# The last mixer's convolution norm: its sums move to GpSimd, its root to columns, its gate behind the head loop

## The chip, the core and the metric

The kernel runs on one core of one Trainium2 chip. The metric is the device time of one execution in microseconds. A core has TensorE (matmuls; its weight loads have a row of their own), VectorE, ScalarE, GpSimd and a queue of transfers; in the traces they are PE (PEld), DVE, ACT, POOL and SP. They run side by side and wait for each other by semaphores.

## What is computed

Two blocks of two layers each over 512 tokens of width 1024, all in float32. The change concerns the odd mixer of the second block, the last one in the program. Its reference, cut to what matters:

```python
def odd_mixer(h, w_in, dw_w, dw_b, ln_g, ln_b, conv_w, conv_b, A_log, dt_bias, D_skip, norm_w, w_out):
...
    g = glu_a * jax.nn.sigmoid(glu_b)
    g = depthwise_conv(g, dw_w, dw_b, CONV_K // 2, CONV_K // 2)
    g = jax.nn.silu(layer_norm(g, ln_g, ln_b))
    xbc = jax.nn.silu(depthwise_conv(xbc, conv_w, conv_b, SSM_CONV // 2, SSM_CONV - 1 - SSM_CONV // 2))
...
    y_f = ssd_scan(xs, dt[:, :, 0], A[0], Bm, Cm)
    y_b = flip(ssd_scan(flip(xs), flip(dt[:, :, 1]), A[1], flip(Bm), flip(Cm)))
    y = (y_f + y_b + xs * D_skip.astype(jnp.float32)[:, None]).reshape(b, S, SSM_INNER)
    y = rms_norm(y * jax.nn.silu(z.astype(jnp.float32)), norm_w).astype(h.dtype)
    return jnp.concatenate([g, y], axis=-1) @ w_out
```

The filter of `g` has 31 taps (CONV_K) on 512 channels, that of `xbc` four on 2048; the scan has 16 heads in four groups.

`layer_norm` subtracts the mean over the 512 channels and multiplies by the reciprocal root of the mean square plus 1e-6.

## The kernel before

Channels lie on the 128 partitions and tokens along the free dimension, so a tile is 128 x 512 and the 512 channels of `g` are four tiles `CO[0]` to `CO[3]`. All projections stream their weights in chunks of 128 output channels: a transfer fills `w_raw`, ScalarE writes the high part (`split_high`, L323), GpSimd the low part (`pool_stream`, L335), and TensorE does three products for each of eight input tiles (`product`, L374). High and low parts have two buffers, so a chunk's high part can be written once the chunk two before it has been multiplied. The order is written out by hand, engine by engine, in `odd_pe`, `odd_act`, `odd_dve` and `pool_stream`; every engine works its list strictly in order.

In the mixer come the chunks of g and its gate, one of dt, 16 of xbc and 8 of z, and then the output product in two parts: `o_out_g` (8 chunks of half depth, from g) and `o_out_y` (8 chunks, from y). Meanwhile the long filter's 31 taps are computed: VectorE (`taps`, L2768) does tiles 0 and 1 and 20 taps of tile 2, with the running sum in PSUM banks 5 and 6; ScalarE writes the products of tile 3 and of the 11 other taps of tile 2 (`tap_terms`, L2368) and GpSimd adds them up (`pool_taps`, L2378). In each chunk's step ScalarE has the high part of the weights first and the products second, GpSimd the low part first and the adds second. `conv_sum` (L2790) and `activated` are the short filter of xbc.

Behind the chunks comes the prologue of the scan: scores of head group 0 (L2469), decay rows of heads 0 and 1 (L2496, L2498), the four column sums of g (L2519), the products carried between token blocks (`carried`, L2482 and L2484), the mean (L2833), the four subtractions (L2836), four squares on ScalarE (L2650) with their sums on TensorE (L2524), mean square (L2840) and root (L2652). Then 16 head steps: ScalarE writes a head's weights (`decays`, L2638), VectorE adds the two directions (L2848) and multiplies by the scores (L2850), TensorE multiplies by x (`pair`, L2530), VectorE finishes a pair of heads (`finish`, L2824 and L2827). In between lie, for each group of four heads, `scaled_rows` (L2807) and `from_carried` (L2817). Reciprocal and scaling of the norm stand in steps 0 and 1 (L2853, L2857), Silu and high parts of g behind ScalarE's step 7 (L2660, L2663), low parts in VectorE's step 10 (L2862). GpSimd only squares the finished y (`pool_squares`, L2385 and L2388). Behind the loop come the sum for y's norm (L2549, L2551), the first part of the output product, the reciprocal (L2877), and y in high and low parts (L2881, L2891).

`YOFF` lies in `rope_sb` and `square_sum`, `CO` and the filter's input in `y_space`, `TERM`, `L_SUM` and the decay weights in `arena`, `XS`, `CBS` and `OM` in `x_space`. G is the PSUM: banks 4 and 5 serve scores and carried products in turn (`ring`).

## Time and profile before

| | us |
|---|---|
| median of 3 runs | 3685.42 |
| lowest, highest run | 3682.53, 3688.09 |
| profiled execution, its own time | 3684.6 |
| its span, first to last instruction | 3682.8 |
| TensorE busy in the span | 3565.9 (97%) |
| VectorE busy | 1784.2 (48%) |
| ScalarE busy | 1278.2 (35%) |
| GpSimd busy | 1492.9 (41%) |
| stretch 3112 to 3135 (prologue of the scan), TensorE busy | 19.53 of 23.00 |
| stretch 3135 to 3208 (head steps), TensorE busy | 59.06 of 73.00 |
| the same, VectorE and ScalarE busy | 61.52 and 46.95 |

Positions in the text are microseconds from the start of the span. The page of the profile gives busy times by engine; the chain of waits follows the work that ended last back to what released it; the timeline lists an engine's instructions in order, with the idle time before one in brackets and the engine that ended it. The span is 1.8 us shorter than the execution's own time.

### The profile page before, as it was taken

How to read it: one execution, taken by the hardware profiler on the slowest of the kernel's cores; microseconds unless marked ns; L12 is line 12 of the kernel's file. 1: busy time of each engine (PE TensorE's matmuls, PEld its weight loads, DVE VectorE, ACT ScalarE, POOL GpSimd, SP SyncE). 2: the span in 40 equal slices, each digit the busy share in tenths (PEclk: the TensorE clock that was granted, in tenths of full speed). 3: DMA queues.
4: the chain of work that ended last, by engine and by line, in shares of the span. 5: the costliest groups of instructions: out<-in, count | busy, mean ns of one | idle time of the engine just before them, and what ended most of it. 6: DMA issues, size and time to landing. Idle time of an engine off the chain costs nothing.

```text
span 3682.8 us, 54791 instructions
## 1 busy us (share of the span) xinstructions
PE 3565.9 (97%) x20592; PEld 3064.8 (83%) x20592; DVE 1784.2 (48%) x2350; ACT 1278.2 (35%) x2142; POOL 1492.9 (41%) x661
## 2 busy tenths in 40 slices
PE   8999999999988999999999999999999999899998
PEld 8988999999966888888887888888888876588886
DVE  3773664447555444632246442335233587753234
ACT  3643332222264222422233532224222455542222
POOL 3331444443402444444452234444444465244443
PEclk9999999999998999999999999999999999999999
DMA  4220222222201222222232112232222222022222
GB/s 147 78 75 30 87 87 92 88 90 87 86 24 46 94 96 95 88 92 91 97 109 75 47 57 97 91 100 89 97 91 97 92 86 69 7 98 94 95 95 82
DMA packets 86428, 307.38 MB, mean 83 GB/s; under 512 B 9568, under 2 KB 11872, under 8 KB 86112
## 3 DMA queue, kind: packets, MB, share of 16 engines
q1 hardware_dynamic: 85824, 303.69, 24.6%
q8 instruction: 135, 2.21, 0.3%
q10 hardware_dynamic: 416, 1.05, 0.1%
q14 instruction: 53, 0.43, 0.0%
HBM read 302.60 MB, written 2.10 MB: 83 GB/s over the span
## 4 chain that ended last, share of the span: by engine, by line
PE 86%; DVE 8%; ACT 3%; DVEq 1%; issue 1%; POOL 0%; DMA 0%; ACTq 0%; SPq 0%; POOLq 0%
PE psum L374 71%; PE psum L586 6%; PE psum L604 1%; DVE arena L1170 1%; PE psum L624 1%; PE psum L2097 1%; DVE arena L1201 1%; PE psum L1308 1%; DVE psum L2790 0%; PE psum L1326 0%; DVE scale L666 0%; PE psum L2061 0%; DVE square_sum L491 0%; PE psum L2081 0%; ACT arena L2638 0%
## 5 line engine op out<-in xcount | busy, mean ns | idle before, releaser
L335 POOL TENSOR_TENSOR w_lo<-w_raw,w_hi 128x1024 fp32r<-128x1024 f32 (+1 forms) x507 | 1262.0, 2490 | 1787.8 <-ACT w_hi L323 1787.7
L323 ACT ACTIVATE w_hi<-w_raw 128x1024 fp32r<-128x1024 f32 (+1 forms) x507 | 533.8, 1053 | 1842.6 <-PE psum L374 1831.4
L374 PE MATMUL psum<-x_hi,w_hi 128*128 128x512 f32 (+1 forms) x2744 | 902.0, 357 | 12.7 <-POOL w_lo L335 8.4
L374 PE MATMUL psum<-x_lo,w_hi 128*128 128x512 f32 (+1 forms) x2744 | 902.6, 357 | 0.0
L374 PE MATMUL psum<-x_hi,w_lo 128*128 128x512 f32 (+1 forms) x2744 | 898.4, 356 | 0.0
L374 PE MATMUL psum<-y_hi,w_hi 128*128 128x264 f32 (+1 forms) x2272 | 634.9, 329 | 11.8 <-DVE arena L1179 3.4
L374 PE MATMUL psum<-y_lo,w_hi 128*128 128x264 f32 (+1 forms) x2272 | 634.3, 329 | 0.0
L374 PE MATMUL psum<-y_hi,w_lo 128*128 128x264 f32 (+1 forms) x2272 | 631.8, 328 | 0.0
L374 PEld LDWEIGHTS psum<-x_hi,w_hi 128*128 128x128 f32 x2744 | 485.4, 188 | 96.3 <-POOL w_lo L335 9.7
L374 PEld LDWEIGHTS psum<-x_lo,w_hi 128*128 128x128 f32 x2744 | 484.5, 188 | 78.7 <-issue 1.4
L374 PEld LDWEIGHTS psum<-x_hi,w_lo 128*128 128x128 f32 x2744 | 485.1, 189 | 76.5
L374 PEld LDWEIGHTS psum<-y_hi,w_hi 128*128 128x128 f32 x2272 | 383.8, 189 | 55.6 <-issue 6.8
L374 PEld LDWEIGHTS psum<-y_lo,w_hi 128*128 128x128 f32 x2272 | 383.0, 189 | 38.9 <-issue 0.5
L374 PEld LDWEIGHTS psum<-y_hi,w_lo 128*128 128x128 f32 x2272 | 383.1, 189 | 38.0
L1045 DVE TENSOR_TENSOR arena<-psum,arena 128x512 f32<-128x512 f32 x88 | 60.9, 692 | 393.8 <-PE psum L374 387.5
L1049 DVE TENSOR_TENSOR y_lo<-arena,y_hi 128x512 f32 x88 | 193.5, 2199 | 90.5 <-ACT y_hi L1017 90.5
L420 DVE TENSOR_TENSOR arena<-psum,scale 128x512 f32<-128x512 f32 (+1 forms) x80 | 55.7, 697 | 296.0 <-PE psum L374 296.0
L335 POOL TENSOR_TENSOR w_resident<-w_raw,w_resident 128x1024 fp32r<-128x1024 f32 (+1 forms) x50 | 108.5, 2191 | 190.8 <-DVE x_lo L874 108.0
L406 DVE TENSOR_TENSOR arena<-psum,scale 128x512 f32 (+3 forms) x68 | 47.0, 697 | 271.5 <-PE psum L374 270.0
L966 DVE TENSOR_TENSOR y_lo<-arena,y_hi 128x528 f32 (+1 forms) x64 | 152.8, 2388 | 18.2 <-ACT y_hi L935 16.8
L1043 DVE TENSOR_TENSOR arena<-psum,scale 128x512 f32<-128x512 f32 x88 | 60.8, 691 | 135.9 <-PE psum L374 134.9
L961 DVE TENSOR_SCALAR arena<-psum 128x528 f32<-128x528 f32 (+1 forms) x64 | 44.8, 699 | 107.9 <-PE psum L374 98.3
(510 smaller groups left out, 4280.8 us busy)
## 6 DMA issues: line engine op xcount, KB each, us to landing
w_raw<-in_weights SPq DMA_DIRECT2D x566, 512.0 KB, 3.3
resid<-in_xT SPq DMA_DIRECT2D x8, 264.0 KB, 8.0
out_dram<-resid SPq DMA_DIRECT2D x16, 128.0 KB, 1.7
arena<-in_lru_w SPq DMA_DIRECT2D x1, 1024.0 KB, 10.1
rope_sb<-in_rope SPq DMA_DIRECT2D x1, 528.0 KB, 11.4
rope_sb<-in_rope ACTq DMA_DIRECT2D x1, 512.0 KB, 4.7
y_space<-in_pool_inv ACTq DMA_DIRECT2D x1, 512.0 KB, 6.1
mats<-in_mats SPq DMA_DIRECT2D x1, 448.0 KB, 10.5
```

Of the source, the lines that this page charges most:

```text
L323: nc.scalar.activation(weight_parts(n, i, c)[0][:, 0:w], RAW[:, (n + c) % 4, 0:w], ACT.Copy).then_inc(high_ready, 1)
L335: nc.gpsimd.tensor_tensor(wl[:, 0:w], RAW[:, (n + c) % 4, 0:w], wh[:, 0:w], ALU.subtract).then_inc(low_ready, 1)
L374: last = mm(o[:, a, :], wt[:, k * P:k * P + P], x[:, k, a * (w // banks):(a + 1) * (w // banks)], start=(k == 0 and p == 0), stop=(k == kt ...
L406: take(dve, n, count, lambda ps, i, c: tt(toks(dst[:, 4 * i + c, offset:offset + w], n), ps, toks(RS[:, 0:w], n), ALU.mult))
L420: tt(toks(t, n), acc(n, c), toks(RS[:, 0:w], n), ALU.mult).then_inc(psum_free, 1)
L586: last = mm(G[:, (n + c) % 4, half(h)], w[:, k * P:k * P + P], x[:, k, half(h)], start=(k == 0 and q == 0), stop=(k == kt - 1 and q == 2))
L604: mm(G[:, 4, half(h)], ones[:, :], PREP_SQ[m % 4], start=(k == 0), stop=(k == DT - 1)).then_inc(wide_summed, 1)
L961: ts(toks(SCR[:, 2 + c % 2, 0:w], n), ps, 0.0, None, ALU.max).then_inc(psum_free, 1)
L966: tt(YL[:, 4 * i + c, 0:w], SCR[:, c % 2, 0:w], YH[:, 4 * i + c, 0:w], ALU.subtract).then_inc(h_low, 1)
L1043: tt(SCR[:, 2 + c // 2, 0:T2], acc(n, c)[:, 0, :], RS[:, 0:T2], ALU.mult).then_inc(psum_free, 1)
L1045: tt(SCR[:, c // 2, 0:T2], acc(n, c)[:, 0, :], SCR[:, 2 + c // 2, 0:T2], ALU.mult).then_inc(psum_free, 1)
L1049: tt(YL[:, 2 * j + c // 2, 0:T2], SCR[:, c // 2, 0:T2], YH[:, 2 * j + c // 2, 0:T2], ALU.subtract).then_inc(h_low, 1)
```

## The change

- The long filter: VectorE does 16 taps of tile 2 in place of 20 and keeps the running sum in `CO[2]` (SBUF) in place of PSUM. GpSimd adds up the other 15 in a scratch tile `PART2`; they start one chunk earlier than its taps did and end two chunks later. VectorE adds `PART2` at the end.
- In all chunk steps of xbc and z ScalarE has its tap products ahead of the high part of the weights, and GpSimd its adds ahead of the low part.
- The sums: GpSimd adds the four tiles of g (`pool_moments`), one matmul sums over the channels, VectorE writes the mean; GpSimd subtracts it from the four tiles, squares and adds the squares, in eleven operations.
- The root: four one-column matmuls put the sums of squares in four columns (tokens on the partitions); VectorE adds the small constant and makes a first guess from the bits; GpSimd refines it by three Newton steps of four operations on 128 x 4 elements, ahead of its second square of y; four matmuls spread the roots over a bank, ScalarE copies it to SBUF ahead of its step 10. No square root and no reciprocal of full tiles is left in this norm.
- The scaling of the four tiles goes to VectorE's steps 10 to 13; Silu, high parts and low parts of g go behind the loop. The first chunk of `o_out_g` stands ahead of the last matmul of y's norm and waits for g's parts tile by tile.
- The order of the two PSUM banks of the ring is shifted once for group 2 and back for group 3, and the scores wait for the bank's new users.

```diff
@@ pool_stream
                     for n in range(a, b):
+                        pool_taps(pool, n - CHUNKS["xbc"] - 3)
+                        if n == CHUNKS["o_out_g"] + 1:
+                            pool_moments(pool)
                         if n == CHUNKS["o_out_g"] + 2:
                             pool_squares(pool)
                         one(n, 0, 0)
-                        pool_taps(pool, n - CHUNKS["xbc"] - 3)
...
+        PART2, L_SUM, L_SQ, L_RSTD = (SCR[:, i, 0:T2] for i in (5, 4, 5, 4))
+        L_VAR, L_ROOT, L_STEP = (COL[:, 96 + 4 * i:100 + 4 * i] for i in range(3))
+
+        def pool_sum(f):
+            return PART2 if f == 2 else CO[f]
+
+        def ring(use):
+
+            return 4 + (use + (use >= 14) + (use >= 21)) % 2
+
+        POOL_TAPS = [(3, j) for j in range(CONV_K)] + [(2, j) for j in range(16, CONV_K)]
...
-                nc.gpsimd.tensor_tensor(CO[f], CO[f], TERM[k % 2], ALU.add).then_inc(st["o_pt"], 1)
+                nc.gpsimd.tensor_tensor(pool_sum(f), pool_sum(f), TERM[k % 2], ALU.add).then_inc(st["o_pt"], 1)
+
+        def pool_moments(pool):
+
+            pool.wait_ge(st["o_gc"], 2)
+            pool.drain()
+            nc.gpsimd.tensor_tensor(L_SUM, CO[0], CO[1], ALU.add)
+            pool.drain()
+            nc.gpsimd.tensor_tensor(L_SUM, L_SUM, CO[3], ALU.add)
+            pool.drain()
+            pool.wait_ge(st["o_gc"], 3)
+            nc.gpsimd.tensor_tensor(L_SUM, L_SUM, CO[2], ALU.add).then_inc(st["o_ln"], 1)
+            pool.wait_ge(st["o_xm"], 1)
+            for f in range(4):
+                nc.gpsimd.tensor_tensor(CO[f], CO[f], MU, ALU.subtract)
+                pool.drain()
+                last = nc.gpsimd.tensor_tensor(GSQ if f else L_SQ, CO[f], CO[f], ALU.mult)
+                pool.drain()
+                if f:
+                    last = nc.gpsimd.tensor_tensor(L_SQ, L_SQ, GSQ, ALU.add)
+                    pool.drain()
+            last.then_inc(st["o_ln"], 1)
 
         def pool_squares(pool):
 
             for f in range(DT - 1):
+                if f == 1:
+                    pool.wait_ge(st["o_xm"], 2)
+                    for _ in range(3):
+                        nc.gpsimd.tensor_tensor(L_STEP, L_ROOT, L_ROOT, ALU.mult)
+                        pool.drain()
+                        nc.gpsimd.tensor_tensor(L_STEP, L_STEP, L_VAR, ALU.mult)
+                        pool.drain()
+                        nc.gpsimd.tensor_scalar(L_STEP, L_STEP, -0.5, 1.5, ALU.mult, ALU.add)
+                        pool.drain()
+                        last = nc.gpsimd.tensor_tensor(L_ROOT, L_ROOT, L_STEP, ALU.mult)
+                        pool.drain()
+                    last.then_inc(st["o_ln"], 1)
...
-        TAP_ORDER = [(f, j) for j in range(1, CONV_K) for f in (0, 1)] + [(2, j) for j in range(20)]
+        TAP_ORDER = [(f, j) for j in range(1, CONV_K) for f in (0, 1)] + [(2, j) for j in range(16)]
...
         def tap_sum(f):
-            return G[:, 6 if f else 5, :]
+            return CO[2] if f == 2 else G[:, 5 + f, :]
@@ odd_pe
-            pe.wait_ge(st["o_gc"], 1)
-            for f in range(4):
-                last = mm(G[:, 6, :], ones[:, :], CO[f], start=(f == 0), stop=(f == 3))
-            last.then_inc(st["o_mu"], 1)
+            pe.wait_ge(st["o_ln"], 1)
+            mm(G[:, 6, :], ones[:, :], L_SUM, start=True, stop=True).then_inc(st["o_st"], 1)
             carried(0)
-            for f in range(4):
-                pe.wait_ge(sq_in, f + 1)
-                mm(G[:, 7, :], ones[:, :], GSQ, start=(f == 0), stop=(f == 3)).then_inc(sum_in, 1)
+
+            def squared_columns():
+
+                pe.wait_ge(st["o_ln"], 2)
+                pe.wait_ge(st["o_oe"], 5)
+                for j in range(NB):
+                    last = mm(G[:, 4, j:j + 1], L_SQ[:, P * j:P * j + P], ones[:, 0:1], start=True, stop=True)
+                last.then_inc(st["o_st"], 1)
+
+            def roots_spread():
+
+                pe.wait_ge(st["o_ln"], 3)
+                pe.wait_ge(st["o_oe"], 8)
+                for j in range(NB):
+                    last = mm(G[:, 4, P * j:P * j + P], L_ROOT[:, j:j + 1].broadcast_to([P, P]), ident[:, :], start=True,
+                              stop=True)
+                last.then_inc(st["o_st"], 1)
...
+                if f == 2:
+                    squared_columns()
+                if f == 4:
+                    roots_spread()
...
             mm(G[:, 4, :], ones[:, :], Y_SUM, start=True, stop=False)
-            pe.wait_ge(sq_in, 4 + 1)
+            n = CHUNKS["o_out_g"]
+            product(pe, n, 1, YH, YL, kt=4, parts=SPLIT_AT["o_g"][0])
+            pe.wait_ge(sq_in, 1)
@@ odd_act
             for c in range(16):
+                tap_terms(act, c - 1)
                 split_high(act, CHUNKS["xbc"] + 2, 0, c)
-                tap_terms(act, c - 1)
...
             decays(0)
             decays(1)
-            act.wait_ge(st["o_xm"], 1)
-            for f in range(4):
-                if f:
-                    act.wait_ge(sum_in, f)
-                nc.scalar.activation(GSQ, CO[f], ACT.Square).then_inc(sq_in, 1)
-            act.wait_ge(var_in, 1)
-            nc.scalar.activation(SCR[:, 5, 0:T2], SCR[:, 4, 0:T2], ACT.Sqrt).then_inc(std_in, 1)
+            split_high(act, CHUNKS["z"] + 2, 0, DT - 1)
             for h in range(2, SSM_HEADS):
+                if h == 10:
+                    act.wait_ge(st["o_st"], 3)
+                    nc.scalar.activation(L_RSTD, G[:, 4, :], ACT.Copy).then_inc(st["o_lc"], 1)
                 decays(h)
                 if h % HG == 2 and h // HG + 1 < SSM_GROUPS:
                     score_copies(h // HG + 1)
-                if h == 7:
-                    act.wait_ge(st["o_g"], 1)
-                    for f in range(4):
-                        nc.scalar.activation(CO[f], CO[f], ACT.Silu, bias=vec("ln_b", f))
-                    act.drain()
-                    for f in range(4):
-                        nc.scalar.activation(YH[:, f, 0:T2], CO[f], ACT.Copy).then_inc(h_high, 1)
+            for f in range(4):
+                act.wait_ge(st["o_g"], f + 1)
+                nc.scalar.activation(CO[f], CO[f], ACT.Silu, bias=vec("ln_b", f))
+                act.drain()
+                nc.scalar.activation(YH[:, f, 0:T2], CO[f], ACT.Copy).then_inc(h_high, 1)
@@ odd_dve
                     dve.wait_ge(st["o_pt"], adds(len(POOL_TAPS)))
-                    tt(CO[2], CO[2], tap_sum(2), ALU.add)
+                    tt(CO[2], CO[2], PART2, ALU.add).then_inc(st["o_gc"], 1)
...
-            dve.wait_ge(st["o_mu"], 1)
-            ts(MU, G[:, 6, :], 1.0 / 512, None, ALU.mult)
-            dve.drain()
-            for f in range(4):
-                last = tt(CO[f], CO[f], MU, ALU.subtract)
-            last.then_inc(st["o_xm"], 1)
+            dve.wait_ge(st["o_st"], 1)
+            ts(MU, G[:, 6, :], 1.0 / 512, None, ALU.mult).then_inc(st["o_xm"], 1)
             from_carried(0)
-            dve.wait_ge(sum_in, 4)
-            ts(SCR[:, 4, 0:T2], G[:, 7, :], 1.0 / 512, EPS, ALU.mult, ALU.add).then_inc(var_in, 1)
             for h in range(SSM_HEADS):
                 g, w, m = h // HG, W[h % 2], OM[h % 2]
+                if h == 4:
+                    dve.wait_ge(st["o_st"], 2)
+                    ts(L_VAR, G[:, 4, 0:NB], 1.0 / 512, EPS, ALU.mult, ALU.add)
+                    dve.drain()
+                    ts(L_ROOT.bitcast(I32), L_VAR.bitcast(I32), -0.5, 1597463007.0, ALU.mult,
+                       ALU.add).then_inc(st["o_xm"], 1)
...
-                if h == 0:
-                    dve.wait_ge(std_in, 1)
-                    nc.vector.reciprocal(SCR[:, 4, 0:T2], SCR[:, 5, 0:T2])
-                if h == 1:
-                    dve.drain()
-                    for f in range(4):
-                        last = stt(CO[f], CO[f], vec("ln_g", f), SCR[:, 4, 0:T2], ALU.mult, ALU.mult)
-                    last.then_inc(st["o_g"], 1)
-                if h == 10:
-                    for f in range(4):
-                        dve.wait_ge(h_high, SPLIT_AT["o_g"][0] + f + 1)
-                        tt(YL[:, f, 0:T2], CO[f], YH[:, f, 0:T2], ALU.subtract).then_inc(h_low, 1)
+                if 10 <= h < 14:
+                    f = h - 10
+                    if f == 0:
+                        dve.wait_ge(st["o_lc"], 1)
+                    stt(CO[f], CO[f], vec("ln_g", f), L_RSTD, ALU.mult, ALU.mult).then_inc(st["o_g"], 1)
...
+            for f in range(4):
+                dve.wait_ge(h_high, SPLIT_AT["o_g"][0] + f + 1)
+                tt(YL[:, f, 0:T2], CO[f], YH[:, f, 0:T2], ALU.subtract).then_inc(h_low, 1)
             finish(DT - 1)
```

ScalarE in the step of xbc chunk 5 before; `y_space` to `arena` are the tap products, `arena` from `arena` is a logarithm for dt:

```order
L2571 ACTIVATE arena<-psum 128x512 [waits o_cv]
L323 ACTIVATE w_hi<-w_raw 128x1024 [waits tile_done,raw_loaded1]
L2368 ACTIVATE arena<-y_space,vecs_sb 128x512 [waits o_pt] x2
L2587 ACT_TABLE_LOAD
L2587 ACTIVATE arena<-arena 128x128 [waits o_dt]
L2594 ACTIVATE psum<-arena,vecs_sb 128x512 [waits o_xe,o_si]
```

and in the change:

```order
L2637 ACTIVATE arena<-psum 128x512 [waits o_cv]
L2379 ACTIVATE arena<-y_space,vecs_sb 128x512 [waits o_pt] x2
L323 ACTIVATE w_hi<-w_raw 128x1024 [waits tile_done,raw_loaded1]
L2653 ACT_TABLE_LOAD
L2653 ACTIVATE arena<-arena 128x128 [waits o_dt]
L2660 ACTIVATE psum<-arena,vecs_sb 128x512 [waits o_xe,o_si]
```

The high part of the weights has moved behind the two products.

GpSimd at the end of the z chunks before; `w_lo` are low parts of the weights, `y_space` from `y_space` and `arena` the adds of taps, `x_space` from `arena` the squares of y:

```order
L335 TENSOR_TENSOR w_lo<-w_raw,w_hi 128x1024
L2378 TENSOR_TENSOR y_space<-y_space,arena 128x512 x2
L335 TENSOR_TENSOR w_lo<-w_raw,w_hi 128x1024 x2
L2385 TENSOR_TENSOR x_space<-arena 128x512 x2
L2388 TENSOR_TENSOR x_space<-x_space 128x512
```

and in the change, up to the first square of g:

```order
L335 TENSOR_TENSOR w_lo<-w_raw,w_hi 128x1024
L2389 TENSOR_TENSOR arena<-arena 128x512 x2
L2395 TENSOR_TENSOR arena<-y_space 128x512
L2397 TENSOR_TENSOR arena<-arena,y_space 128x512
L2400 TENSOR_TENSOR arena<-arena,y_space 128x512
L2403 TENSOR_TENSOR y_space<-y_space,scale 128x512
L2405 TENSOR_TENSOR arena<-y_space 128x512
L2403 TENSOR_TENSOR y_space<-y_space,scale 128x512
```

The adds go on for two chunks longer, and the sums of g stand between them and the last low part.

VectorE from the last add of the filter to step 1 before; `x_space` from `arena` 128x1024 are scaled rows, the pairs of `x_space` 128x512 the head steps, `rope_sb` and `square_sum` the reads of carried products:

```order
L2774 TENSOR_TENSOR y_space<-y_space,psum 128x512
L2807 TENSOR_TENSOR x_space<-arena 128x1024 x3
L2833 TENSOR_SCALAR scale<-psum 128x512
L2836 TENSOR_TENSOR y_space<-y_space,scale 128x512 x4
L2817 TENSOR_TENSOR rope_sb<-psum,arena 128x512 x2
L2817 TENSOR_TENSOR square_sum<-psum,arena 128x512
L2840 TENSOR_SCALAR arena<-psum 128x512
L2848 TENSOR_TENSOR x_space<-arena 128x512
L2850 TENSOR_TENSOR x_space<-x_space 128x512
L2853 RECIPROCAL arena<-arena 128x512
L2848 TENSOR_TENSOR x_space<-arena 128x512
L2850 TENSOR_TENSOR x_space<-x_space 128x512
```

and in the change:

```order
L2835 TENSOR_TENSOR y_space<-y_space,arena 128x512
L2867 TENSOR_TENSOR x_space<-arena 128x1024 x3
L2892 TENSOR_SCALAR scale<-psum 128x512
L2876 TENSOR_TENSOR rope_sb<-psum,arena 128x512 x2
L2876 TENSOR_TENSOR square_sum<-psum,arena 128x512
L2907 TENSOR_TENSOR x_space<-arena 128x512
L2909 TENSOR_TENSOR x_space<-x_space 128x512
L2907 TENSOR_TENSOR x_space<-arena 128x512
L2909 TENSOR_TENSOR x_space<-x_space 128x512
L2867 TENSOR_TENSOR x_space<-arena 128x1024 x3
```

The subtractions, the mean square, the reciprocal and the scaling are gone from here.

## Rows read from the trace of the kernel before

**Rows 1.** Chain of waits: start us, us, engine, buffer, line, count.
```profile
3116.68 3.45 PE psum L2519 x8
...
3243.41 18.48 PE psum L374 x78
```

**Rows 2.** Stretches: window, its us, busy us and count per engine, PEclk, DMA share, GB/s.
```profile
3072.00:3076.00 4.00, 3.72 (x12) 3.15 (x13) 3.76 (x6) 3.30 (x6) 2.69 (x2) 0.57 0.03 6
3112.00:3135.00 23.00, 19.53 (x64) 10.11 (x64) 14.39 (x20) 13.33 (x33) 1.67 (x1) 1.00 0.06 23
3135.00:3208.00 73.00, 59.06 (x369) 40.28 (x367) 61.52 (x73) 46.95 (x148) 19.16 (x13) 0.98 0.00 1
```

**Rows 3.** Timeline, GpSimd and VectorE: start us, us, engine, line, operation, count.
```profile
3220.29 2.96 POOL L335 TENSOR_TENSOR w_lo<-w_raw,w_hi 128x512 fp32r<-128x512 f32 x2 [3.98 <-ACT w_hi L323]
...
3222.20 1.60 DVE L2881 SCALAR_TENSOR_TENSOR arena<-arena,vecs_sb 128x512 f32<-128x512 f32 x1
...
3238.79 2.99 DVE L2881 SCALAR_TENSOR_TENSOR arena<-arena,vecs_sb 128x512 f32<-128x512 f32 x1
...
3238.83 2.40 POOL L335 TENSOR_TENSOR w_lo<-w_raw,w_hi 128x1024 fp32r<-128x1024 f32 x1 [0.68 <-ACT w_hi L323]
```

**Rows 4.** One line's instructions: duration ns minimum, median, maximum; first, last start.
```profile
L2768 DVE SCALAR_TENSOR_TENSOR psum<-y_space,vecs_sb,psum x77: 748/755/759, 2962.1 to 3114.2; 128x512 f32<-128x512 f32 x77
```

**Rows 5.** Timeline of ScalarE, GpSimd, TensorE, VectorE around xbc chunks 7 and 10.
```profile
2995.91 1.06 ACT L323 ACTIVATE w_hi<-w_raw 128x1024 fp32r<-128x1024 f32 x1 [0.17 <-issue]
...
2996.87 1.32 ACT L2368 ACTIVATE arena<-y_space,vecs_sb 128x512 f32<-128x512 f32 x2
...
2997.04 2.35 POOL L335 TENSOR_TENSOR w_lo<-w_raw,w_hi 128x1024 fp32r<-128x1024 f32 x1 [7.60 <-ACT w_hi L323]
...
2999.45 0.79 PE L374 MATMUL psum<-x_hi,w_hi 128*128 128x512 f32 x1 [6.60 <-POOL w_lo L335]
...
3025.63 0.69 DVE L2782 TENSOR_TENSOR arena<-psum,scale 128x512 f32<-128x512 f32 x1 [0.19 <-PE psum L374]
```

**Rows 6.** Timeline, end of the z chunks: GpSimd add, VectorE taps, last eviction.
```profile
3103.34 1.28 POOL L2378 TENSOR_TENSOR y_space<-y_space,arena 128x512 f32<-128x512 f32 x1 [0.16 <-issue]
...
3104.91 4.91 DVE L2768 SCALAR_TENSOR_TENSOR psum<-y_space,vecs_sb,psum 128x512 f32<-128x512 f32 x6
...
3110.12 0.69 DVE L2796 TENSOR_TENSOR y_space<-psum,scale 128x512 f32<-128x512 f32 x1 [0.31 <-PE psum L374]
```

**Rows 7.** Timeline of TensorE: behind an idle time; first and last carried products of group 0.
```profile
3072.28 1.09 PE L2446 MATMUL psum<-ident,arena 128*128 128x128 f32 x4 [5.21 <-ACT arena L2602]
...
3119.95 0.59 PE L2482 MATMUL psum<-x_space 128*128 128x256 f32 x2
...
3125.53 0.59 PE L2484 MATMUL psum<-x_space 128*128 128x256 f32 x2
```

**Rows 8.** Timeline of VectorE: head steps 0, 1, 4 and 15.
```profile
3133.17 0.68 DVE L2848 TENSOR_TENSOR x_space<-arena 128x512 f32<-128x512 f32 x1
...
3134.53 3.35 DVE L2853 RECIPROCAL arena<-arena 128x512 f32<-128x512 f32 x1
...
3139.28 2.74 DVE L2857 SCALAR_TENSOR_TENSOR y_space<-y_space,vecs_sb,arena 128x512 f32<-128x512 f32 x4
...
3154.13 0.69 DVE L2848 TENSOR_TENSOR x_space<-arena 128x512 f32<-128x512 f32 x1 [0.40 <-PE psum L2530]
...
3203.39 1.37 DVE L2850 TENSOR_TENSOR x_space<-x_space 128x512 f32<-128x512 f32 x1
```

**Rows 9.** Timeline of VectorE (step 8, step 10, behind the loop); line L521 on TensorE.
```profile
3173.06 0.69 DVE L2848 TENSOR_TENSOR x_space<-arena 128x512 f32<-128x512 f32 x1 [1.05 <-ACT arena L2638]
...
3183.78 2.49 DVE L2862 TENSOR_TENSOR y_lo<-y_space,y_hi 128x512 fp32r<-128x512 f32 x4
...
3214.85 3.34 DVE L2877 RECIPROCAL arena<-arena 128x512 f32<-128x512 f32 x1
...
L521 PE MATMUL psum<-ones,square_sum x38: 238/250/261, 23.2 to 1193.3; 128*128 128x1 f32 x38
```

56 lines of the change are left out of this document (28 added, 28 removed).

## The prediction

> **What bounds the kernel now.** I began with the busy shares: TensorE 97%, so over the span the matmuls are the bound and only a stretch where TensorE waits can move the end. The chain of waits shows where that is near the change: while the last mixer's convolutions are formed, it runs through VectorE; in the scan's prologue it goes through the four column sums of the norm (the first of [rows 1]), then through the squares, which ScalarE and TensorE do in turn; from there it goes through the 16 head steps and a norm to 3243.41, where the output product at last runs without a wait (the second of [rows 1]). In the stretches of the table TensorE is 85% busy in the prologue (19.53 of 23.00 us) and 81% in the head steps, while VectorE has 61.52 of 73.00 us [rows 2]. So the head steps go by VectorE and the hand-overs round it, not by matmuls. GpSimd has 19.16 us there, and the change gives it more. That makes the meeting of VectorE and GpSimd the question.
>
> **What they do to each other.** Two halves of a split (1.29 us each) took 2.96 us together when a VectorE instruction came between them; that VectorE instruction and the one behind it were held until GpSimd ended: 1.60 us where 0.75 is usual, and 2.99 us against a split of 2.40 us [rows 3]. Both read two tensors from SBUF. The convolution's multiply-add with its running sum in PSUM never shows it: 77 of them lie between 748 and 759 ns though GpSimd's adds (1.28 us, the next one 0.16 us behind [rows 6]) and splits run all through that stretch [rows 4]. So an instruction with both inputs in SBUF takes turns with GpSimd. Price of a turn: with a 1.29 us operation the pair takes 2.96 - 1.29 = 1.67 us where VectorE alone needs 4.91/6 = 0.82 [rows 6], so +0.85; with a 2.40 us split, by the same 1.67 - 1.29 = 0.38, 2.40 + 0.38 - 0.82 = +1.96.
>
> The Trainium skill (SBUF — State Buffer, Who interferes with whom) states the same lock for two SBUF inputs and speaks against this change in one more point: it counts only the inputs, so moving a tap's running sum out of PSUM is enough to bring the lock in. By that rule the term for the taps below is 8.7 us; without it that term is nothing.
>
> **Part 1, order of weights and taps.** Every step now issues ScalarE's tap products ahead of its high part of the weights, and GpSimd's two adds ahead of the low part. Mostly the products run while ScalarE would wait for TensorE anyway. At 2995.91 they can't: ScalarE is late, its high part is at once followed by GpSimd's low part, and TensorE, idle for 6.60 us, starts at 2999.45 [rows 5]. Now the first product is ready at 2995.91 + 0.7 = 2996.6, two adds take 2 x (1.29 + 0.16) = 2.9 us [rows 6], the low part 2.35: TensorE starts at 3001.9, +2.5 us. The next chunks have slack against VectorE, but at 3025.63 VectorE waits 0.19 us for TensorE [rows 5], and behind it the chain is VectorE's. Term: **+2.5**. Bounds: 0 (if the start hides) and 2.9.
>
> **Part 2, taps.** VectorE's taps of tile 2 go from 20 to 16 (-4 x 0.82 = -3.3 us at the end), but all now have both inputs in SBUF: 3 in the step of z chunk 4, 6 in each of chunks 5 and 6, one tap and the final add in the last. Against the 15 ahead of the eviction of chunk 7 stand six adds, one sum and two splits: 7 x 0.85 + 2 x 1.96 = 9.8 us, less 1.1 us of idle time ahead of three evictions (0.31 ahead of the last [rows 6]): 8.7. The eviction of chunk 7 goes from 3110.12 [rows 6] to 3118.8. ScalarE's Silu of that chunk, the score copies and the decay rows hang on it.
>
> **Part 3, prologue.** Removed from its path: three of the four sums (3.45 us for four, 0.86 each [rows 1]), the four subtractions, four squares and four sums of squares, the mean of squares. TensorE reached the sums 3116.68 - 3110.12 = 6.6 us behind the eviction; now 3118.8 + 6.6 = 3125.4, plus 0.86 for the one sum, plus the carried products, 3119.95 to 3126.12 = 6.2 us [rows 7], plus 0.7 for VectorE's last read: the first head step at 3133.2, where it was 3133.17 [rows 8]. So everything gained is spent on the taps. TensorE is now idle for some 6 us before the scores; behind the 5.21 us of idle time that ended at 3072.28 the granted clock was 0.57 for 4 us, near the lower of its two levels, 1.2 GHz [rows 2, 7]. That costs 0 to 1.7 us; I take **+0.8**. The sum on GpSimd waits for the last tap; it is done before TensorE asks.
>
> **Part 4, head steps 0 to 3.** They took 3154.13 - 3133.17 = 20.96 us [rows 8]. Out: the reciprocal 3.35 and the scaling 2.74 (-6.1). In: GpSimd's eleven operations on means and squares begin when the mean is written, 6.3 us before the first head step; at 1.45 us each four are over, seven are left. The seven VectorE instructions of steps 0 and 1 and of the scaled rows, all with two SBUF inputs, pay 7 x 0.85 = 6.0; then one split (+1.96) and the first square (+0.6): 8.6. At step 4 VectorE waits for four one-column matmuls (0.25 us each [rows 9]) and does two small instructions: +1.5. GpSimd's wait for this blocks the squares of y behind it, which have the rest of the loop. Term: -6.1 + 8.6 + 1.5 = **+4.0**. Bounds: -4.6 (no turn taken) and +6.5 (each turn priced as 2.99 - 0.75 = 2.24 for splits and 1.3 for the rest).
>
> **Part 5, the rest of the loop.** ScalarE's Silu and casts leave the loop: the 1.05 us that VectorE waited at 3173.06 go [rows 9], -1.05. Twelve small GpSimd operations: +0.7 by turns. At step 10 four low parts (2.49) go, two scalings of 0.75 come: -1.0. Two more in steps 12 and 13, one in idle time: +0.8. The spread of roots falls into ScalarE's former delay: 0. Sum **-0.55**.
>
> **Part 6, behind the loop.** Four Silu and four casts now follow the last decay, beside VectorE's last products, but the four low parts (2.49 us [rows 9]) stand ahead of the last finish and partly wait for ScalarE: I take 2.2 us. Against that the reciprocal no longer waits for a chunk of the output product: it started 3214.85 - 3204.76 = 10.1 us behind the last head step (3203.39 + 1.37 [rows 8]); now 3.1 for the finish as before, 2.2 for the push, 3.4 for square, sum, mean and root of 0.6 to 1.0 each: 8.7. Term: **-1.4**; bounds -3 and +2.
>
> **Sum.** 2.5 + 0.8 + 4.0 - 0.55 - 1.4 = +5.35 us. The profiled execution is 3684.6 us (span 3682.8); 3684.6 + 5.4 = 3690. The median of the runs, 3685.4, is 0.8 us above it; I leave that to the range. The clock, here 0.98 to 1.00 in the loop and prologue [rows 2], is taken as unchanged but for the 0.8.
>
> **Rivals.**
> (A) *The taps take no turn*, because VectorE gets in between GpSimd's operations: the eviction stays at 3110.12, TensorE has no long idle time ahead of the scores, the loop still pays. Time: 3690 - 8.7 - 0.8 = 3680.5. Against it: every two-input row beside a GpSimd one is held.
> (B) *Neither pays*: also part 4's 8.6 goes: 3672. Only if the held rows had another cause; no row speaks for it.
> (C) *The roots come too late*, slower. GpSimd is asked for a reciprocal square root in twelve operations, between step 4 and the spread ahead of step 10's decays, about 19 us (3154.13 to 3173). It has no row for so small an operation nor for a scalar one. Between 0.16 and 1.45 us each (the gap alone, a whole 128x512 add) the twelve need 2 to 17 us; it decides from 19 us on: then TensorE stands in front of the decays and each microsecond counts in full. With the first scalar operation costing as much as several adds, 8 us late: 3698. The Trainium skill (GPSIMD Engine Reference, Instruction dispatch) names about 6 us for the first call of freshly loaded code, and the order shows a load ahead of this first scalar operation; by that price alone, 6 + 12 x 0.5, it would still fit, and the sum stays.
> (D) *The wait of part 1 is hidden*: 3687.5, within the forecast's own range.
>
> **How the numbers follow.** The forecast with D (3684 to 3696): 60%. A: 16%, B: 7%, C: 17%. A measurement of this kernel can tell 0.2%, 7.4 us, from no change: below 3678.0 is faster, above 3692.8 slower. Faster: B and 5 of A: 12%. Same: 42 of the forecast, 11 of A, 2 of C: 55%. Slower: 18 of the forecast, 15 of C: 33%. Range 3677 to 3699: leaves out B and the end of A below, the far half of C above.
>
> **What would show it.** Taps of tile 2 in SBUF at 1.3 to 2.9 us in place of 0.75, and chunk 7's eviction 8 to 9 us later against the chunks' product; TensorE's start at 2999 moved by 2.5; the two-input instructions of steps 0 and 1 at 1.3 to 1.7 us; 25 us from step 0 to 4; the reciprocal 8.7 us behind the last step. The forecast is wrong if the taps keep 0.75 us, if the first head step comes before 3130, or if TensorE stands in front of step 10's decays.

## The result, and the profile after

| | before | after |
|---|---|---|
| median of 12 runs, us | 3685.19 | 3692.25 |
| lowest, highest run | 3682.53, 3688.09 | 3687.95, 3696.70 |
| ratio, 95% interval | | 1.0016 (1.0008 to 1.0023) |
| profiled execution: span, mean granted clock | 3682.8, 0.992 | 3691.1, 0.988 |
| head steps, from step 0 to the end of step 15 | 71.59 | 77.26 |

After is 7.06 us slower: less than the 0.2% that this kernel's measurement can tell apart, though the interval excludes equal times. 3690 was forecast. That the sum came out is worth little by itself, since two of its terms were wrong by 2 us and more in opposite directions. So the traces are compared term by term.

The program ahead of the stage is the same in both, yet the stage begins at different positions, so all positions are counted from VectorE's first read of xbc chunk 0. These two rows of the timeline (start us, us, engine, line, operation, output and inputs, shape, count) are that point, of before and of after:

```profile
2961.33 0.69 DVE L2782 TENSOR_TENSOR arena<-psum,scale 128x512 f32<-128x512 f32 x1
...
2962.50 0.69 DVE L2843 TENSOR_TENSOR arena<-psum,scale 128x512 f32<-128x512 f32 x1
```

| us | before | after | difference | forecast | after, second profile |
|---|---|---|---|---|---|
| first read to eviction of z chunk 2 | 118.77 | 118.66 | -0.1 | +2.5 (part 1) | 119.10 |
| z chunk 2 to z chunk 7 | 30.02 | 38.06 | +8.0 | +8.7 (part 2) | 38.07 |
| z chunk 7 to head step 0 | 23.05 | 14.15 | -8.9 | -8.7 +0.8 (part 3) | 14.44 |
| head step 0 to 4 | 20.96 | 24.92 | +4.0 | +4.0 (part 4) | 24.92 |
| head step 4 to the end of 15 | 50.63 | 52.34 | +1.7 | -0.55 (part 5) | 52.34 |
| to the reciprocal | 10.09 | 10.17 | +0.1 | -1.4 (part 6) | 8.71 |
| to the uninterrupted output product | 28.56 | 29.87 | +1.3 | 0 | 28.60 |
| to the end of the span | 439.39 | 440.43 | +1.0 | 0 | 438.92 |
| sum | 721.47 | 728.60 | +7.1 | +5.35 | 725.10 |

The last column is a profile of the same kernel after, taken with the experiments below. By it the stage is 3.6 us longer than in before, not 7.1: its head steps agree, what follows them does not. Before has one profile, so a difference of 1 us in a row of this table rests on one execution on each side.

**Part 1.** TensorE's timeline in after, at the late low part and at the next long idle time (the brackets give the idle time before a row and what ended it), and VectorE's eviction of z chunk 2 in before and in after:

```profile
3002.88 0.79 PE L376 MATMUL psum<-x_hi,w_hi 128*128 128x512 f32 x1 [6.58 <-POOL w_lo L335]
...
3074.93 0.63 PE L2490 MATMUL psum<-ident,arena 128*128 128x128 f32 x4 [2.59 <-ACT arena L2668]
...
3080.10 0.69 DVE L2796 TENSOR_TENSOR y_space<-psum,scale 128x512 f32<-128x512 f32 x1 [3.85 <-PE psum L374]
...
3081.16 0.69 DVE L2857 TENSOR_TENSOR y_space<-psum,scale 128x512 f32<-128x512 f32 x1 [2.25 <-PE psum L376]
```

TensorE starts 40.38 us behind the first read where it was 38.12, so the wait forecast as 2.5 is there with 2.3 [rows 5]. But TensorE's wait behind the last xbc chunk, which ends with a tile from ScalarE (L2668), fell from 5.21 [rows 7] to 2.59 us. It ends 112.43 us behind the first read, 1.5 us later than in before (110.95), so part of the delay is still there. The work from there to the eviction took 7.82 us in before, where the granted clock was 0.57 from 3072 to 3076 [rows 2], and takes 6.23 us in after at 1.00: 1.6 us come back by the clock, and VectorE's wait at z chunk 2 is as much shorter (3.85 and 2.25 us). The second profile of after has the restart 0.4 us late and 7.79 us of work behind it, the six experiments that leave both orders as in after have 1.1 to 1.4 and 6.2 us. What became of the rest of the 2.3 us stands at p1_old_order below.

**Part 2.** VectorE's taps of tile 2 beside z chunks 5 and 6, and the evictions of chunks 6 and 7; before had 4.91 us for six taps and the last eviction at 3110.12 [rows 6]:

```profile
3101.16 10.04 DVE L2829 SCALAR_TENSOR_TENSOR y_space<-y_space,vecs_sb 128x512 f32<-128x512 f32 x6
3111.12 0.68 DVE L2857 TENSOR_TENSOR y_space<-psum,scale 128x512 f32<-128x512 f32 x1
3111.89 7.41 DVE L2829 SCALAR_TENSOR_TENSOR y_space<-y_space,vecs_sb 128x512 f32<-128x512 f32 x6
3119.22 0.68 DVE L2857 TENSOR_TENSOR y_space<-psum,scale 128x512 f32<-128x512 f32 x1
```

A tap takes 10.04 / 6 = 1.67 us on average, beside two adds and parts of two splits (L335 at 3100.37 and 3106.37); single ones of the 15 taps in SBUF take 0.75 to 2.75 us.

**Part 3.** TensorE at the scores and at the one column sum, and VectorE's first head step:

```profile
3121.27 3.67 PE L2516 MATMUL psum<-arena 128*128 128x512 f32 x4 [4.99 <-ACT x_space L2694]
...
3126.53 1.02 PE L2565 MATMUL psum<-arena,ones 128*128 128x512 f32 x2
...
3133.37 0.68 DVE L2907 TENSOR_TENSOR x_space<-arena 128x512 f32<-128x512 f32 x1
```

The one sum stands where four stood [rows 1]. Step 0 starts 0.2 us behind its old position in the span [rows 8], and 1.0 us ahead of it when both are counted from the first read. The four scores take 3.67 us where they took 1.98 in before (L2469 at 3112.95), behind 4.99 us of idle time: TensorE ran near 1.2 GHz there (granted clock 0.64 from 3112 to 3121, 0.79 from 3121 to 3130). The sum so comes 7.31 us behind the eviction of z chunk 7 where 6.56 was worked out, 0.75 us late. The carried products take 5.3 us (3127.39 to 3132.72) where they took 6.2 with a wait of 0.60 us for VectorE among them.

**Part 4.** Steps 2 and 4 on VectorE, and GpSimd's last add of squares and the split beside step 2:

```profile
3145.16 1.75 DVE L2907 TENSOR_TENSOR x_space<-arena 128x512 f32<-128x512 f32 x1
3146.99 2.69 DVE L2909 TENSOR_TENSOR x_space<-x_space 128x512 f32<-128x512 f32 x1
...
3157.92 0.16 DVE L2898 TENSOR_SCALAR columns<-psum 128x4 f32<-128x4 f32 x1 [1.31 <-PE psum L2573]
...
3144.30 2.06 POOL L2408 TENSOR_TENSOR arena<-arena,x_space 128x512 f32<-128x512 f32 x1
3146.52 2.61 POOL L335 TENSOR_TENSOR w_lo<-w_raw,w_hi 128x1024 fp32r<-128x1024 f32 x1 [0.16 <-issue]
```

Each of VectorE's two instructions stands until the one of GpSimd is over: 3146.99 + 2.69 and 3146.52 + 2.61 end 0.55 us apart. Step 4's columns wait 1.31 us for TensorE.

**Part 5.** GpSimd's squares of y behind the Newton steps with the two VectorE instructions beside them, and the same meeting at the gate of step 11:

```profile
3166.88 1.04 POOL L2429 TENSOR_TENSOR x_space<-arena 128x512 f32<-128x512 f32 x1 [0.16 <-issue]
3168.07 1.53 POOL L2432 TENSOR_TENSOR x_space<-x_space 128x512 f32<-128x512 f32 x1
...
3167.18 1.29 DVE L2907 TENSOR_TENSOR x_space<-arena 128x512 f32<-128x512 f32 x1 [1.21 <-issue]
3168.54 1.60 DVE L2909 TENSOR_TENSOR x_space<-x_space 128x512 f32<-128x512 f32 x1
...
3192.02 1.53 POOL L2432 TENSOR_TENSOR x_space<-x_space 128x512 f32<-128x512 f32 x1
3192.34 1.75 DVE L2914 SCALAR_TENSOR_TENSOR y_space<-y_space,vecs_sb,arena 128x512 f32<-128x512 f32 x1
```

**Part 6.** VectorE's four low parts and the last finish, the reciprocal, and TensorE's mean and the start of the uninterrupted product:

```profile
3210.55 3.56 DVE L2924 TENSOR_TENSOR y_lo<-y_space,y_hi 128x512 fp32r<-128x512 f32 x4
3214.04 0.73 DVE L2883 SCALAR_TENSOR_TENSOR arena<-arena,vecs_sb,psum 128x512 f32<-128x512 f32 x1
...
3220.80 3.35 DVE L2932 RECIPROCAL arena<-arena 128x512 f32<-128x512 f32 x1
...
3218.36 1.02 PE L2617 MATMUL psum<-arena,ones 128*128 128x512 f32 x2
...
3250.67 0.54 PE L376 MATMUL psum<-x_hi,w_hi 128*128 128x512 f32 x1 [2.31 <-DVE x_lo L2946]
```

The low parts push the last finish to 3214.04, 3.4 us behind the last step's end at 3210.63 (it was 1.6). The last square is ready at 3216.2, but TensorE adds it at 3218.36, behind the first chunk of the output product.

### The profile page after: what moved, and what is told of

It is laid out like the page before. It is cut to its first block, busy times and chain, and to the rows that moved or that the text cites. A ratio compares the mean times of both kernels' runs of the same rounds, so it can differ in the third digit from the quotient of the medians.

```text
span 3691.1 us, 54846 instructions
## 1 busy us (share of the span) xinstructions
PE 3569.9 (97%) x20594; PEld 3068.6 (83%) x20594; DVE 1795.2 (49%) x2342; ACT 1275.2 (35%) x2139; POOL 1528.1 (41%) x691
## 3 DMA queue, kind: packets, MB, share of 16 engines
q10 hardware_dynamic: 416, 1.05, 0.1%
## 4 chain that ended last, share of the span: by engine, by line
PE 85%; DVE 9%; ACT 2%; DVEq 2%; issue 1%; POOL 0%; DMA 0%; ACTq 0%; SPq 0%; POOLq 0%
PE psum L376 70%; PE psum L588 6%; PE psum L606 1%; DVE arena L1172 1%; PE psum L626 1%; PE psum L2099 1%; DVE psum L2851 1%; DVE arena L1203 1%; DVE y_space L2829 1%; PE psum L1310 1%; PE psum L1328 0%; DVE scale L668 0%; PE psum L2063 0%; DVE arena L2936 0%; DVE psum L2829 0%
## 5 line engine op out<-in xcount | busy, mean ns | idle before, releaser
L335 POOL TENSOR_TENSOR w_lo<-w_raw,w_hi 128x1024 fp32r<-128x1024 f32 (+1 forms) x507 | 1263.8, 2493 | 1756.7 <-ACT w_hi L323 1756.6
L376 PE MATMUL psum<-x_hi,w_hi 128*128 128x512 f32 (+1 forms) x2744 | 903.3, 358 | 17.6 <-POOL w_lo L335 11.8
L335 POOL TENSOR_TENSOR w_resident<-w_raw,w_resident 128x1024 fp32r<-128x1024 f32 (+1 forms) x50 | 108.7, 2196 | 190.7 <-DVE x_lo L876 108.0
```

The source lines that it names most:

```text
L335: nc.gpsimd.tensor_tensor(wl[:, 0:w], RAW[:, (n + c) % 4, 0:w], wh[:, 0:w], ALU.subtract).then_inc(low_ready, 1)
L376: last = mm(o[:, a, :], wt[:, k * P:k * P + P], x[:, k, a * (w // banks):(a + 1) * (w // banks)], start=(k == 0 and p == 0), stop=(k == kt ...
```

## The experiments

Each was timed against before on the same chip. The expectations of the first set call the eviction at 3080.10 (before) and 3081.16 (after) that of z chunk 1; it is chunk 2's. What the expectation of p4_split_early calls the last square is GpSimd's last add of squares (L2408).

| run | ratio to before, 95% | first read to uninterrupted product | step 0 to 4 |
|---|---|---|---|
| before | 1 | 282.1 | 20.96 |
| after (again) | 1.0016 (1.0007, 1.0025) | 286.2 | 24.92 |
| p1_old_order | 1.0006 (0.9997, 1.0015) | 287.9 | 26.49 |
| p2_sum_psum | 0.9987 (0.9978, 0.9996) | 280.6 | 27.22 |
| b_sum_sbuf | 1.0027 (1.0016, 1.0038) | 291.3 | 21.18 |
| p4_one_moment | 0.9997 (0.9988, 1.0006) | 285.2 | 23.80 |
| p6_mean_first | 1.0012 (1.0003, 1.0021) | 286.6 | 24.91 |
| p4_split_early | 1.0010 (1.0001, 1.0019) | 284.5 | 22.59 |
| newton9 | 1.0027 (1.0017, 1.0038) | 291.6 | 24.92 |
| c_all | 0.9979 (0.9970, 0.9988) | 275.6 | 22.77 |
| c_all_old | 0.9972 (0.9961, 0.9984) | 274.1 | 22.75 |

**after_again: the kernel after, unchanged.**

> The kernel after itself, unchanged, in the same set as the variants. The stage from VectorE's first read of xbc chunk 0 to the uninterrupted output product takes 288.2 us again, within 0.3; the part ahead of it is the same work in each kernel and began the stage anywhere from 2961.3 to 2965.5 us in six profiles. If the median is 7 us over before again (1.0019), the three variants of the first set that lay 3 to 5 us under what their traces add up to did so by that part; if it is 2 to 4 us over before (1.0008), the comparison of sets was off by as much.

The median is 3692.43 us, the ratio again 1.0016. The stage was expected within 0.3 us and is 2.0 us shorter: up to the end of step 15 the second profile agrees with the first to 0.7 us, and what differs is behind it. Its reciprocal and its uninterrupted product:

```profile
3223.08 3.35 DVE L2932 RECIPROCAL arena<-arena 128x512 f32<-128x512 f32 x1
...
3251.68 0.50 PE L376 MATMUL psum<-x_hi,w_hi 128*128 128x512 f32 x1 [0.76 <-DVE x_lo L2946]
```

8.71 us from the last step to the reciprocal where the first profile has 10.17, and 28.60 from there to the product where it has 29.87. The two stretches of 4 us behind the last step, first profile and second (its us, busy us of PE, PEld, DVE, ACT, POOL, granted clock, DMA):

```profile
3210.63:3214.63 4.00, 3.94 (x19) 2.58 (x20) 4.00 (x6) 1.79 (x3) 1.13 (x1) 0.50 0.00 0
3214.63:3218.63 4.00, 4.00 (x14) 3.12 (x13) 0.83 (x2) 1.91 (x2) 0.00 (x0) 0.72 0.00 0
...
3214.37:3218.37 4.00, 3.94 (x21) 2.77 (x22) 4.00 (x6) 1.79 (x3) 1.14 (x1) 0.61 0.00 0
3218.37:3222.37 4.00, 4.00 (x17) 2.94 (x16) 1.52 (x3) 1.92 (x2) 0.00 (x0) 1.00 0.00 0
```

With the same work TensorE was granted 0.50 and 0.72 in the one and 0.61 and 1.00 in the other. Behind the reciprocal the turns fall otherwise too: of the last six scalings (L2936) the first profile has all held at 1.60 to 2.98 us, the second has four at 0.75. So a single profile decides nothing of 3 us behind the loop, while the head steps of these two repeat to 0.05 us. That is no rule either: in p1_old_order the same steps take 1.6 us more. The three variants of the first set with medians 3 to 5 us under what their traces add up to are not explained by a comparison that is off for all kernels. One reason is on record: their profiled executions were slow ones among their own runs, p1_old_order with 3693.47 us against a median of 3688.57, p2_sum_psum with 3688.35 against 3683.17, p4_one_moment with 3690.12 against 3687.34.

**p1_old_order: part 1 undone.**

```diff
             for c in range(16):
-                tap_terms(act, c - 1)
                 split_high(act, CHUNKS["xbc"] + 2, 0, c)
+                tap_terms(act, c - 1)
```

and `pool_taps` behind the low part in the same steps of GpSimd.

> The kernel after, with the weights' high parts ahead of the tap products again, and the low parts ahead of GpSimd's adds, in the 16 steps of the xbc chunks only (part 1 undone; the z steps as after). Theory of the prediction: TensorE's late start (3002.88 in after, 2999.45 before) goes back by 2.5 us and everything behind it too: median about 3689.8. Rival: the trace of after has the eviction of z chunk 1 at 3081.16 against 3080.10, no later than the whole stage already began (3.4 us at 3002.88 were down to 1.06), because TensorE's clock between 3072 and 3084 was 1.00 where before it was 0.86 behind a 5.21 us idle time; then undoing the order brings that idle time and the slow clock back and the time stays at 3692, within 1 us, with z chunk 1 evicted no earlier against the stage's start.

TensorE's start goes back by 2.3 us against the first read (38.11), as both theories had it:

```profile
3001.63 0.80 PE L379 MATMUL psum<-x_hi,w_hi 128*128 128x512 f32 x1 [6.59 <-POOL w_lo L335]
...
3081.52 0.69 DVE L2860 TENSOR_TENSOR y_space<-psum,scale 128x512 f32<-128x512 f32 x1 [2.26 <-PE psum L379]
```

VectorE from the small instructions for dt to its next read, in p1_old_order and then in after:

```profile
3033.41 0.22 DVE L2788 COPY arena<-psum 128x64 f32<-128x64 f32 x1 [0.16 <-issue]
...
3036.91 1.30 DVE L2799 TENSOR_TENSOR arena<-arena 128x48 f32<-128x48 f32 x1
...
3040.19 0.69 DVE L2846 TENSOR_TENSOR arena<-psum,scale 128x512 f32<-128x512 f32 x1 [0.17 <-issue]
...
3035.33 0.22 DVE L2785 COPY arena<-psum 128x64 f32<-128x64 f32 x1 [0.16 <-issue]
...
3039.83 0.69 DVE L2843 TENSOR_TENSOR arena<-psum,scale 128x512 f32<-128x512 f32 x1 [0.17 <-issue]
```

The eviction of z chunk 2 comes 118.00 us behind the first read, 0.7 less than in after; the wait there is 2.26 us as in after. The trace thus gives 0.7 us of the 2.5, the ratios 3.7 with an interval of some 4. Over all profiles of the changed kernel that eviction comes 118.3 to 119.1 us behind the first read with the new order (eight of them) and 118.0 and 117.4 with the old.

The second pair of rows shows where the delay went. It does reach VectorE: the copy L2788 comes 69.89 us behind the first read, L2785 in after 72.83, so 2.9 us. But these small instructions read two tensors from SBUF, and GpSimd's operations hold three of them in p1_old_order (2.42, 1.30 and 1.32 us) and one in after (2.22). To the next read it is 6.78 us against 4.50, and 0.7 us of delay are left. All eight profiles with the new order have 4.5 us there, the two with the old 6.8 and 5.6, before 5.6.

The rival is half right. The clock is what covers the 1.5 us that TensorE's restart is late in after against before. But undoing the xbc steps brings neither the long idle time (2.40 us) nor the slow clock back; so it is not their order that made the idle time short. Which of the other edits did, no run sets apart. Steps 2 to 4 took 14.70 us where after has 13.13, with the last two carried products at 1.02 us where after has 0.59 and the product of the heads behind them at 1.98 where after has 1.09; that spoils its total of 287.9. The pair c_all and c_all_old below repeats the question: 1.5 us by the trace, 1.1 by the medians' differences to before, 2.6 by the ratios.

**p2_sum_psum and b_sum_sbuf: one operand's memory, in each direction.**

```diff
         def tap_sum(f):
-            return CO[2] if f == 2 else G[:, 5 + f, :]
+            return G[:, 6 if f else 5, :]
...
-                    tt(CO[2], CO[2], PART2, ALU.add).then_inc(st["o_gc"], 1)
+                    tt(CO[2], tap_sum(2), PART2, ALU.add).then_inc(st["o_gc"], 1)
```

> The kernel after, with the running sum of tile 2's taps on VectorE in PSUM bank 6 again (16 taps; the last add takes the PSUM sum and GpSimd's partial sum and writes the tile). One input of each tap is then in PSUM. Theory (turns at SBUF): taps at 0.75 us, from the eviction of z chunk 1 to that of chunk 7 30.0 us in place of 38.06, everything behind 8 us earlier: first head step 14.1 us behind the eviction as in after, 25 us from step 0 to step 4; median 3684 to 3685. Rival (the taps were not what held the evictions, something else in the z stage was): 38 us stays, median 3692. A second rival: the evictions are 8 us earlier but the first head step is not, since something else in the prologue ends last then (GpSimd's adds, the state products): first head step 18 us or more behind the eviction, median 3688 or more.

b_sum_sbuf is the same edit of the kernel before in the other direction. Its 20 taps and four sums stay; GpSimd's partial sum of tile 2, which lay in `CO[2]`, moves to another SBUF tile to make room.

> The kernel before, with one thing changed: tile 2's running sum on VectorE is in SBUF (GpSimd's partial sum of that tile moved to another SBUF buffer to make room), all 20 taps and the four column sums as before. Theory (turns): 15 taps, six adds and the splits between the evictions of z chunk 1 and 7 make 38.7 us of the 30.0; the last 5 taps and the sum have less beside them, +1; the prologue behind it unchanged: first head step 9 to 10 us later, median 3685.2 + 9.5 = 3694.7. Rival (no turn, or cover in the prologue): 3685, within 1.5 us.

Six taps beside z chunk 5 and the last eviction with the sum in PSUM, then six with it in SBUF in the kernel before:

```profile
3102.57 4.90 DVE L2829 SCALAR_TENSOR_TENSOR psum<-y_space,vecs_sb,psum 128x512 f32<-128x512 f32 x6
3113.78 0.69 DVE L2857 TENSOR_TENSOR y_space<-psum,scale 128x512 f32<-128x512 f32 x1 [0.32 <-PE psum L376]
...
3100.14 10.03 DVE L2768 SCALAR_TENSOR_TENSOR y_space<-y_space,vecs_sb 128x512 f32<-128x512 f32 x6
```

The same shape takes 4.90 us and 10.03 us (10.04 and 4.91 in the kernels that they were made from), and nothing of VectorE's work but the place of the sum was changed. The evictions of chunks 2 to 7 take 30.0 us in p2_sum_psum (38.1 in after) and 37.5 in b_sum_sbuf (30.0 in before); the times move by -10.7 us (0.9987 against 1.0016) and +10.0 (1.0027), the stage by -7.5 (280.6 against 288.2) and +9.2. The turns of the taps are shown, the rival without turns has fallen, and so has the second rival: step 0 comes 12.67 us behind the eviction, not 18. In p2_sum_psum the head steps give 2.3 us back, and one row says where 1.4 of it is:

```profile
3147.69 2.90 PE L2529 MATMUL psum<-x_space 128*128 128x256 f32 x6 [2.58 <-DVE rope_sb L2876]
```

The carried products run near 1.2 GHz (granted clock 0.60 from 3147.69 to 3151.70): 2.90 us where after has 1.53. Step 4 comes that much later. The idle time ahead of them does not tell the two apart: it is 2.58 us here and was 2.71 in after, where they ran at full clock.

**p4_one_moment: less work on GpSimd in the head steps.** GpSimd centres and squares tile 0 alone; tiles 1 to 3 stay uncentred and their squares are missing.

```diff
-            for f in range(4):
+            for f in range(1):
                 nc.gpsimd.tensor_tensor(CO[f], CO[f], MU, ALU.subtract)
```

> The kernel after, but GpSimd centres and squares only tile 0 of the four (nine of its eleven operations of 1.0 to 2.1 us left out; tiles 1 to 3 are then not centred and their squares are missing from the variance). Theory (turns in the head steps): two GpSimd operations are over before the first head step, what is left beside steps 0 to 3 is one low part; from step 0 to step 4 16.3 to 18 us in place of 24.92; median 3692.2 - 8 = 3684.5. Rival (the head steps are held by something else, the scores or ScalarE's exponentials, which are the same here): 24 us stays, median 3692.

The expectation was far off: 23.80 us from step 0 to 4, not 16.3 to 18. TensorE's four scores, VectorE's step 2, and the stretch (its us, busy us of PE, PEld, DVE, ACT, POOL, granted clock, DMA):

```profile
3139.30 3.78 PE L2516 MATMUL psum<-arena 128*128 128x512 f32 x4 [2.90 <-ACT x_space L2694]
...
3146.70 0.69 DVE L2907 TENSOR_TENSOR x_space<-arena 128x512 f32<-128x512 f32 x1 [5.60 <-ACT arena L2704]
...
3139.00:3146.00 7.00, 6.70 (x26) 4.48 (x28) 2.10 (x2) 4.50 (x16) 0.00 (x0) 0.55 0.00 0
```

VectorE finished the scaled rows at 3141.1, 4.1 us before after does, and then stood 5.60 us. The profile names ScalarE, whose weights were ready at 3145.95. What ended last was the product of the first two heads on TensorE (L2590, 3145.50 to 3146.59), and that stands behind the scores and the state transposes at a granted clock of 0.55. In before the same TensorE chain, at full clock, ended 10.0 us behind step 0. So two paths of nearly equal length run side by side in steps 0 to 2: VectorE's, 11.8 us with the turns, and TensorE's, 10.0 us in before, 11.2 in after and 13.0 here, by its clock. That the clock is the difference is read from rows, no run sets it. In this profile, taking away VectorE's turns alone bought 1.1 us. The runs say more: the ratio is 0.9997 against after's 1.0016, 7 us less with an interval of some 4, which is near the theory's 8, and the profiled execution was 2.8 us slower than the median one. So the second path is shown, and how often it takes the gain away is not.

**p4_split_early: the split out of step 2's way.** GpSimd's split moves ahead of the centring, VectorE's column instructions behind step 4's pair.

```diff
                         if n == CHUNKS["o_out_g"] + 1:
-                            pool_moments(pool)
+                            pool_total(pool)
                         if n == CHUNKS["o_out_g"] + 2:
+                            pool_moments(pool)
                             pool_squares(pool)
...
             score_copies(0)
+            split_high(act, CHUNKS["z"] + 2, 0, DT - 1)
             act.wait_ge(st["o_gc"], 3)
             decays(0)
             decays(1)
-            split_high(act, CHUNKS["z"] + 2, 0, DT - 1)
```

> The kernel after, with GpSimd's weight split moved from behind its centring and squaring to ahead of them (into the 5 us in which it waits for the mean; ScalarE's high part moves ahead of the decays for it), and VectorE's two instructions on the columns moved from ahead of head step 4 to behind its pair. Theory: in after steps 2 to 3 take 5.87 us because two VectorE instructions take turns with the split and the last square (1.75 and 2.69 us), before 2.81; and step 4 waits 1.31 us for the columns. Both go: steps 0 to 4 in 20.9 to 21.5 us where after has 24.92, the first head step at most 0.5 us later; median 3.5 us under after's in the same set. Rival: TensorE's scores, state products and its lower clock set the end of these steps, as in the run with one tile centred (23.80 us there): 24 us, nothing gained.

22.59 us from step 0 to 4, so 2.3 of the 3.5 to 4 expected. VectorE's step 2 and step 4, and GpSimd's split:

```profile
3142.41 0.98 DVE L2905 TENSOR_TENSOR x_space<-arena 128x512 f32<-128x512 f32 x1 [0.71 <-ACT arena L2708]
3143.47 0.69 DVE L2907 TENSOR_TENSOR x_space<-x_space 128x512 f32<-128x512 f32 x1
...
3151.81 0.69 DVE L2905 TENSOR_TENSOR x_space<-arena 128x512 f32<-128x512 f32 x1 [0.40 <-PE psum L2594]
...
3122.62 2.35 POOL L335 TENSOR_TENSOR w_lo<-w_raw,w_hi 128x1024 fp32r<-128x1024 f32 x1 [3.56 <-ACT w_hi L323]
```

Step 2's instructions are at 0.98 and 0.69, step 4 no longer waits for the columns (9.40 us from step 2 to 4 against 13.13). From step 0 to 2 it is 13.19 us against 11.79. The split ends as the centring begins, which so starts 4.3 us ahead of step 0 and not 5.0, and VectorE reaches the end of its scaled rows 0.6 us later. Then it stands 0.71 us: the product of the first two heads ends at 3142.31, 13.09 us behind step 0, at a granted clock of 0.58 from 3135 to 3142. That is TensorE's path again, as long as in p4_one_moment. The median is 2.8 us under after's.

**newton9: the margin of the roots.** Nine Newton steps for three.

> The kernel after with nine Newton steps in place of three: 36 small GpSimd operations, not 12. In after the twelve take 8.3 us (0.19 to 1.04 each) and end 10.6 us before TensorE reaches the spread of the roots. Theory: 24 more take 12 to 17 us; the roots come 2 to 6 us late, TensorE and with it the head steps stand there for as long, part of it given back by the waits that follow; the squares of y behind them have time. 2 to 6 us over after. Rival (the roots have more room than the row says, since the steps that follow wait for VectorE): no change. Second rival (turns between the small operations and VectorE set a price of their own): over 8 us.

The 36 operations take 18.9 us (3159.38 to 3178.29), 0.53 each. A Newton operation and the three scaled rows beside it; TensorE at the spread of the roots; the next scaled rows, and one of the squares of y beside them:

```profile
3164.86 0.99 POOL L2418 TENSOR_TENSOR columns<-columns 128x4 f32<-128x4 f32 x1
3163.45 3.49 DVE L2867 TENSOR_TENSOR x_space<-arena 128x1024 f32<-128x1024 f32 x3
...
3178.34 1.16 PE L2581 MATMUL psum<-ident,columns 128*128 128x128 f32 x8 [0.91 <-POOL columns L2424]
...
3183.49 6.47 DVE L2867 TENSOR_TENSOR x_space<-arena 128x1024 f32<-128x1024 f32 x3
3184.84 1.84 POOL L2429 TENSOR_TENSOR x_space<-arena 128x512 f32<-128x512 f32 x1
```

The small operations hold VectorE nowhere: the scaled rows beside them take 3.49 us for three, as alone in before, and it is GpSimd that is held (0.99 where 0.20 is its shortest). TensorE waits 0.91 us for the roots, so the margin in after was near the 10.6 us read off. The cost is elsewhere: the squares of y, kept waiting by the roots, run without gaps from 3178.45 on and hold step 9 and the next scaled rows (6.47 us, 4.56 in after); from step 8 to 10 it is 3.0 us more. From step 10 to 12 another 1.4 us come from the clock: the carried products at 3197.89 take 2.90 us for 1.53. Against that, steps 5 to 8 are 0.9 us shorter, since no square of y meets them. The median is 5.3 us over after's (4.1 by the ratios), inside the 2 to 6 expected, by another mechanism than the expected one.

**p6_mean_first: behind the loop.** The last finish ahead of the low parts, TensorE's mean ahead of the first output chunk, the reciprocal ahead of the copy of that chunk.

```diff
+            finish(DT - 1)
             for f in range(4):
                 dve.wait_ge(h_high, SPLIT_AT["o_g"][0] + f + 1)
...
-            finish(DT - 1)
...
-            product(pe, n, 1, YH, YL, kt=4, parts=SPLIT_AT["o_g"][0])
             pe.wait_ge(sq_in, 1)
...
+            product(pe, n, 1, YH, YL, kt=4, parts=SPLIT_AT["o_g"][0])
```

> The kernel after, with three edits behind the loop: VectorE finishes the last two heads before the four low parts (not behind them), TensorE takes the mean of squares before the first chunk of the output product (not behind it), and VectorE's reciprocal no longer stands behind the copy of that chunk. Theory from the trace of after: the reciprocal comes 10.17 us behind the last head step because the low parts push the last finish by 3.6 us and the mean then sits 2.1 us behind TensorE's product at the lower clock; without both 7.7 us, and the output product behind it as much earlier: 2.5 us less, median 2 to 3 us under after's in the same set. Rival: the product that now starts later (the low parts come later) or the weight splits beside the scalings are what ends last; then the reciprocal is early and the uninterrupted product isn't: 0.

TensorE's mean and VectorE's reciprocal:

```profile
3215.85 2.07 PE L2616 MATMUL psum<-arena,ones 128*128 128x512 f32 x2 [0.29 <-ACT arena L2727]
...
3219.35 3.35 DVE L2931 RECIPROCAL arena<-arena 128x512 f32<-128x512 f32 x1 [0.70 <-ACT arena L2729]
```

The mean's last matmuls start 0.29 us behind the square that they need (in after 2.1), and the reciprocal 7.83 us behind the last step, as worked out. From there to the uninterrupted product it is 30.65 us against 28.60 and 29.87: VectorE's scalings and GpSimd's splits meet there, and the scalings take up to 2.97 us. Over the stage little of the gain is left: 286.6 us against 288.2 and 286.2 in the two profiles of after. The median is 2.6 us under after's in the same set, but the intervals overlap. So the earlier reciprocal is shown, an earlier end is not, and the rival stands.

**c_all and c_all_old: what the experiments point to.** The edits of p2_sum_psum, p4_split_early and p6_mean_first together; c_all_old has that of p1_old_order too.

> The kernel after with three edits together: tile 2's running sum in PSUM, the three edits behind the loop, and the two of the run p4_split_early. Theory: the gains add in part: 7.5 us by the taps, 2.5 us behind the loop, 3.5 to 4 us in steps 0 to 4: from VectorE's first read of the stage to the uninterrupted output product 275 us where after has 288.2 and before 282.1; about 6 us under before, median near 3680. Rival (each is only cover for the next, TensorE's chain with its clock sets the head steps): only the taps' part stays, 280.6, median as p2_sum_psum.

> The kernel c_all with part 1 undone too: the weights' high parts ahead of the tap products and the low parts ahead of GpSimd's adds in the 16 steps of the xbc chunks. By the trace of p1_old_order the stage's first half gains 0.7 us by it (the eviction of z chunk 2 at 118.00 us behind VectorE's first read against 118.6), by its median 3.7. Theory of the trace: 0.7 us under c_all, which this measurement can't tell from nothing (ratio to before 0.9979 less 0.0002). Theory of the prediction's part 1 (a late start of TensorE goes through in full): 2.5 to 3.7 us under c_all, ratio to before 0.997. From VectorE's first read to the uninterrupted product 275 us in both cases within 1.5, since the clock behind the loop varies by as much.

c_all: median 3678.07 us, 7.9 under before in the same set; 275.6 us from first read to product, the 275 of the theory. c_all_old: 3678.24 with before at 3687.20, ratio 0.9972. Both beat before and after, so the change pays once the running sum stays in PSUM (that edit alone, p2_sum_psum, has 0.9987). The saved sums, squares and reciprocal are then worth more than the turns that remain. Whether c_all_old is better than c_all can't be told by these intervals.

## Why the prediction was right in its sum, and where not

- **Part 1 was mis-sized: +2.5 forecast, between 0 and 0.7 measured (1.1 to 1.5 in the combination).** The late start was right (2.3 us), and it did pass to VectorE. Wrong was to carry it to the end behind "behind it the chain is VectorE's": the chain was followed to chunk 10 and no further. By the traces 2.3 of 2.9 us came back at dt's small instructions, where the new order spares VectorE two turns, and against before the rest was covered by TensorE's clock, which the sum takes as unchanged there. Rival D was nearer. The medians do not exclude the 2.5.
- **Part 2 held.** 8.0 of 8.7 us. The last eviction comes 156.7 us behind the first read, 3118.8 would be 157.5. That the average tap has the 1.67 us priced for one beside an add is chance, since the average holds splits and free taps too. Two runs with one operand moved show the cause. The rule of the Trainium skill (SBUF — State Buffer, Who interferes with whom) that only inputs count fits both runs: the sum's move out of PSUM alone made 4.91 us into 10.03. As input and output move together in them, that the output alone does not count is read from a row of after: two taps that read PSUM and write SBUF (L2829 at 3094.61) take 0.74 and 0.75 us beside a split (L335, 3094.36 to 3096.77).
- **Part 3 was 1.0 us too dear:** -8.9 us measured for -7.9. The clock did fall and made the column sum 0.75 us late, as priced. What was priced too high are the carried products, with 6.2 us taken from a row that has a wait in it; they took 5.3.
- **Part 4 held in its number, and not quite in its reason.** It said -6.1, +8.6, +1.5. From step 0 to 2 the rows give -0.4, from 2 to 3 +3.1, from 3 to 4 +1.3, which fits -6.1 + 6.0, 2.6 and 1.5. But it counts turns as if VectorE were the only path, and p4_one_moment shows a second one, TensorE's, which ends 0.6 us ahead of VectorE's in after (L2590 at 3144.55, step 2 at 3145.16). The lower bound of -4.6 was therefore not to be had: with VectorE's turns gone step 2 still came 13.1 us behind step 0 in p4_one_moment. Rival B, which drops all 8.6, has the held rows against it: 1.75 and 2.69 us at step 2.
- **Part 5 failed: -0.55 forecast, +1.7 measured.** The Newton turns priced +0.7 don't exist; instead the operations delay the squares of y into step 6 and 7 (+1.05 from step 5 to 7). The 1.05 us of ScalarE's Silu came as 0.8. Of the -1.0 for steps 10 and 11 only 0.1 came: step 10 is 1.75 us shorter, step 11 1.67 longer, with a gate that turned with a square (1.75 us for 0.75), which the prediction did not price. Steps 12 to 15 cost 1.5, not 0.8.
- **Part 6: -1.4 to the reciprocal forecast; one profile gives +0.1 and the next -1.4.** The push of the low parts was there (1.8 us more). Left out was that TensorE's last sum stands behind the output chunk, by 2.1 us in the first profile, where the clock is low longer. Behind the reciprocal the forecast had 0; the first profile has +2.3 us against before, the second -0.4.
- **Rival C** did not come: the twelve operations took 8.3 us within its 2 to 17. Its deciding point, 19 us, is close to what newton9 gives (18.9 us, TensorE waits 0.91), but its price is not TensorE's stand, it is the work queued behind on GpSimd. The 6 us that the Trainium skill (GPSIMD Engine Reference, Instruction dispatch) names for a first call are in no row: the first scalar operation took 0.19 us, 0.23 behind the one before. The trace has a record of the load (MODIFY_POOL_CONFIG, twice, 0.11 us ahead of that operation in all ten profiles of the changed kernel), behind the 5.79 us of idle time. So no wait of 6 us follows it here; whether the code lay ready before, no run shows.
- **Luck.** The sum was +5.35 for +7.1 in the first profile and +3.6 in the second. It came that near because errors of -2.6, -0.7 and -1.0 us in parts 1 to 3 stood against +2.3 and +1.5 in parts 5 and 6 and +2.3 behind them.

Open: how much part 1 costs between 0 and 2.5 us; how often TensorE's path, by its clock, takes away what VectorE gains in steps 0 to 2; and what sets that clock, since idle times of the same length (2.58 and 2.71 us) were followed by either level.

## What to carry over

Before moving a running sum out of PSUM, count how many of its instructions will have both inputs in SBUF and what GpSimd does beside them: here that one operand cost what the whole edit saved. Follow a delay past the first place where it bites: here most of it came back at VectorE's small two-input instructions, and a shorter idle time of TensorE gave clock back. Price an engine's relief against the second longest path, since both were within 2.2 us here. Set a profiled execution against the median of its own runs before reading 3 us out of it. Ask of each operation put on an engine's queue what is held behind it; that was dearer than the operation itself.

## What was not expected of the hardware

The same kernel is granted another clock from one execution to the next: 0.72 and 1.00 over the same 4 us of work in two profiles of after, which differ by 4.2 us from the last head step to the end though their head steps agree to 0.05 us; 1.3 of the 4.2 us lie behind the reciprocal, where the turns of scalings and splits fell otherwise. The part of the program ahead of the stage, the same in all kernels, took from 2958.7 to 2965.5 us in twelve profiles, which is about the spread of the runs.

GpSimd operations of 128 x 4 elements did not lengthen VectorE's instructions with two SBUF inputs (three scaled rows 3.49 us, as alone), while these lengthened them from 0.20 to 0.99 us. GpSimd operations of 128 x 512 did lengthen a 128 x 512 instruction, by up to 1.1 us (1.75 for 0.69), and a split of 128 x 1024 by 2.0 us (2.69 for 0.69).
